# In the expert stage ScalarE rounds all weights and GpSimd only gathers token rows

## What is computed

```
def expert_block(args):
    xb, e = args                                   # 128 token rows, one expert
    hb = jax.nn.silu(xb @ w_gate[e]) * (xb @ w_up[e])
    return hb @ w_down[e]
...
y = lax.map(expert_block, (x_pad, blk_expert))
```

## Time and profile before

| what | value |
|---|---|
| median of 3 runs | 3372.45 us |
| lowest, highest | 3366.57, 3375.68 us |
| the profiled execution, own time | 3378.69 us |
| its span, first to last instruction | 3377.0 us |
| mean granted TensorE clock | 0.90 of full speed |
| busy over the span: PE, DVE, POOL, ACT | 2772.1, 1813.5, 895.6, 883.2 us |
| mean DMA traffic over the span | 130 GB/s |
| first expert stage, from the first load to the next stage's | 1074.7 to 1387.4 us |
| second expert stage | 2899.6 to 3328.8 us |

### The profile page before, as it was taken

One profiled execution on the slowest core, in us unless ns is written; L12 is line 12 of the kernel. 1 busy time (PEld: TensorE's weight loads), 2 busy tenths in 40 slices (PEclk: granted clock), 3 DMA queues, 4 the chain that ended last, 5 costly groups with the idle time before them and its releaser, 6 DMA issues. The chain is left out here.

```text
span 3377.0 us, 36221 instructions
## 1 busy us (share of the span) xinstructions
PE 2772.1 (82%) x11986; PEld 2088.9 (62%) x11986; DVE 1813.5 (54%) x1973; ACT 883.2 (26%) x1395; POOL 895.6 (27%) x692
## 2 busy tenths in 40 slices
PE   5897998999894888368997788888999969488883
PEld 4896665776674767247553455557777758377762
DVE  4394672222234878541365567663654362678884
ACT  3012331000121444221243223321222221134441
POOL 1241002222121676311000000003223211366662
PEclk9898898999996999669898789899999989699996
DMA  2110102111043899835022112112111132599999
GB/s 83 39 44 13 26 20 69 34 40 50 31 151 130 314 352 354 320 111 199 19 67 71 43 53 61 42 44 64 43 37 46 35 114 94 196 355 358 367 352 359
DMA packets 223123, 439.13 MB, mean 130 GB/s; under 512 B 22104, under 2 KB 141224, under 8 KB 215112
## 3 DMA queue, kind: packets, MB, share of 16 engines
q1 hardware_dynamic: 201736, 360.57, 31.4%
q0 software_dynamic: 12960, 47.19, 3.7%
q10 hardware_dynamic: 8352, 30.41, 2.2%
HBM read 343.58 MB, written 90.21 MB: 128 GB/s over the span
## 5 line engine op out<-in xcount | busy, mean ns | idle before, releaser
L1786 DVE TENSOR_TENSOR moe_run_w_low<-moe_run_w,moe_run_w_high 128x2048 fp32r<-128x2048 f32 x174 | 449.0, 2587 | 92.7 <-POOL moe_run_w_high L1646 92.6
L1646 POOL CAST moe_run_w_high<-moe_run_w 128x2048 fp32r<-128x2048 f32 x116 | 300.8, 2600 | 193.6 <-DMA moe_run_w<-w_up 108.9
L134 PE MATMUL rnn_ps<-uT_again_high,rnn_w_high 128*128 128x512 f32 x512 | 206.3, 403 | 29.5 <-ACT rnn_gate L2040 16.0
L134 PE MATMUL rnn_ps<-uT_again_low,rnn_w_high 128*128 128x512 f32 x512 | 203.4, 397 | 0.0
L134 PE MATMUL rnn_ps<-uT_again_high,rnn_w_low 128*128 128x512 f32 x512 | 203.0, 397 | 0.0
L1191 DVE TENSOR_TENSOR merge_gated<-merge_branch,merge_gate 128x512 f32<-128x512 f32 x48 | 33.2, 692 | 304.9 <-ACT merge_gate L1176 304.9
L1675 PE MATMUL moe_run_up<-moe_run_w_high,moe_run_xT_high 128*128 128x512 f32 x464 | 196.5, 423 | 0.0
L1675 PE MATMUL moe_run_up<-moe_run_w_low,moe_run_xT_high 128*128 128x512 f32 x464 | 190.0, 409 | 0.0
L1675 PE MATMUL moe_run_up<-moe_run_w_high,moe_run_xT_low 128*128 128x512 f32 x464 | 189.2, 408 | 0.0
L1661 PE MATMUL moe_run_turn<-all_ident,moe_run_x 128*128 128x128 f32 x464 | 77.6, 319 | 130.7 <-DMA moe_run_x<-v,moe_run_idx 130.6
L134 PE MATMUL merge_gates<-uT_high,merge_wg_high 128*128 128x512 f32 x384 | 171.1, 446 | 13.4 <-POOL merge_wg_low L147 13.4
(11 more groups left out here) (442 smaller groups left out, 6769.3 us busy)
## 6 DMA issues: line engine op xcount, KB each, us to landing
moe_run_w<-exp_w SPq DMA_DIRECT2D x96, 512.0 KB, 7.9
moe_run_w<-w_gate SPq DMA_DIRECT2D x68, 512.0 KB, 7.2
moe_run_w<-w_up SPq DMA_DIRECT2D x68, 512.0 KB, 9.0
moe_run_w<-w_down SPq DMA_DIRECT2D x34, 1024.0 KB, 7.3
moe_y<-moe_run_y ACTq DMA_DIRECT2D x58, 512.0 KB, 6.7
moe_run_w<-exp_w SPq DMA_DIRECT2D x24, 1024.0 KB, 7.1
rnn_raw<-w_in SPq DMA_DIRECT2D x32, 512.0 KB, 3.9
moe_y<-moe_run_zero SPq DMA_DIRECT2D x26, 512.0 KB, 8.7
```

The lines of the kernel that those rows point to most:

```text
L134: last = pe.matmul(out, a, b, start=(k == 0), stop=(k == n - 1))
L1646: pool.tensor_copy(hi[p][j][:], raw[p][j][:]).then_inc(s_hi[j], 1)
L1786: dve.tensor_tensor(lo[p][j][:], raw[p][j][:], hi[p][j][:].bitcast(F32), ALU.subtract).then_inc(s_lo[j], 1)
```

## The change

GpSimd's `gather_and_round` becomes `gather`: it copies the row numbers and issues the gather, and no longer casts. The wait for the turned rows of block b - 2 stays, so a gather is issued as soon as its row buffer is free. ScalarE gets the function `round_up`, with the same waits that GpSimd had for these casts (the raw tile loaded; the products that read the previous contents of the high tile done). In its loop the cast of tile 0 of b + 2 comes first, the cast of tile 1 of b + 2 after `round_rows`, and `round_down` of b + 1 moves from the front of the pass to behind the gate. In the prologue the casts of blocks 0 and 1 stand among the casts of rows, ahead of the first `round_down`. The orders on SP, TensorE and VectorE are as before, and VectorE still waits for `s_hi[j]`.

```diff
--- before.py
+++ after.py
@@ -1627,7 +1627,7 @@
 
             @block.gpsimd
             def _(pool):
-                def gather_and_round(i, p, first):
+                def gather(i, p, first):
                     b = 2 * i + p
                     if not first:
                         pool.wait_ge(s_turn, 2 * b - 2)
@@ -1638,13 +1638,7 @@
                     pool.indirect_dma_start(
                         out=x[p][:], out_offset=None, in_=v_d,
                         in_offset=bass.IndirectOffsetOnAxis(ap=idx[p][:, 0:1], axis=0)).then_inc(s_x[p], 16)
-                    for j, s_used in enumerate((s_half, s_up)):
-                        pool.wait_ge(s_raw[p][j], 32 * i + 32)
-                        if not first:
-                            pool.wait_ge(s_used, b - 1)
-                        pool.sem_inc(s_go, 1)
-                        pool.tensor_copy(hi[p][j][:], raw[p][j][:]).then_inc(s_hi[j], 1)
-                in_order(pool, gather_and_round)
+                in_order(pool, gather)
 
             @block.tensor
             def _(pe):
@@ -1720,6 +1714,12 @@
                 for p in range(2):
                     act.sem_inc(s_st[p], ST0)
 
+                def round_up(i, p, j, first=False):
+                    act.wait_ge(s_raw[p][j], 32 * i + 32)
+                    if not first:
+                        act.wait_ge((s_half, s_up)[j], 2 * i + p - 1)
+                    act.copy(hi[p][j][:], raw[p][j][:]).then_inc(s_hi[j], 1)
+
                 def round_down(i, p, first=False):
                     b = 2 * i + p
                     act.wait_ge(s_raw[p][2], 16 * i + 16)
@@ -1756,18 +1756,24 @@
                     act.wait_ge(s_y, 2 * b + 2 + Y0)
                     act.dma_start(y_d[bass.ds(b * P, P), :], y[p][:]).then_inc(s_st[p], 16)
 
+                round_up(0, 0, 0, True)
                 round_rows(0, 0, True)
+                round_up(0, 0, 1, True)
                 round_rows(0, 1, True)
+                round_up(0, 1, 0, True)
+                round_up(0, 1, 1, True)
                 round_down(0, 0, True)
                 gate(0, 0, True)
                 n = more(act)
                 with act.Fori(0, n) as i:
                     for p in range(2):
                         nxt = (i + p, 1 - p)
-                        round_down(*nxt)
+                        round_up(i + 1, p, 0)
                         round_middle(i, p)
                         round_rows(i + 1, p)
+                        round_up(i + 1, p, 1)
                         gate(*nxt)
+                        round_down(*nxt)
                         store(i, p)
                 round_down(n, 1)
                 round_middle(n, 0)
```

## The result

| | before | after |
|---|---|---|
| median of 4 runs each | 3369.51 us | 3312.83 us |
| lowest, highest | 3365.38, 3375.68 | 3306.35, 3317.87 |
| span of the profiled execution | 3377.0 us | 3304.6 us |

The ratio is 0.9829, 95% interval 0.9804 to 0.9854: 57 us faster, where 45 were forecast. On one of the chips (the first run of early gathers alone, gathers behind the second cast, middle first, down cast first, and the kernel before beside them) part of the executions were in a slower state and are left out of the ratios; the traced one of down cast first is among them, and most of its loss lies ahead of the first expert stage, which it reaches at 1137.9 us where middle first does at 1080.6.

What follows compares the result with a forecast made beforehand. The prediction took the DMA engines to bound the expert stages, with 5% left open; -24.6 us in the steady state and -20 at the starts made -45, so 3334 us profiled or 3327 as median, range 3275 to 3362.

Steps and rivals of the forecast that it cites:

- forecast case: Expert stages: steady blocks and starts both gain, -45 us in all, own range -25 to -65; chance 0.50.
- DMA engines as the bound, 5% open, left open by a loop from landing to reload: Steady expert blocks: DMA share 0.95; landing to next issue falls from 14.15 to 10.8 us, loop to 10.3 per block.
- VectorE freed of GpSimd: VectorE's weight differences: all at 2.28 us once GpSimd no longer casts beside them, an excess of 53 us.
- ScalarE fits, 9.4 to 9.7 us, its waits turn into waits for loads: ScalarE per steady block: with the added casts 9.4 to 9.7 us, below 11.66, its groups waiting for weights, not TensorE.
- the layout: One steady block on ScalarE and VectorE, timed from half 0's landing: copies and store to 9.7, loads issued at 10.8 us.
- At the rate of now: Steady blocks: share 0.99 instead of 0.95 at unchanged transfer rate gives 11.39 and 11.19 us, 24.6 us less.
- the two ends: Steady state: near end, today's rate at share 0.99, 24.6 us less; other end, the loop's 10.3 us at 407 GB/s, 75 less.
- faster transfers too: Rival, steady blocks: a queue never dry moves more per busy us, periods 10.3 to 10.7, 75 to 95 us less; chance 0.17.
- The start, -20 us: Starts of both expert stages: earlier second gather and first reload remove nearly all of the idle 10.6 and 9.4 us.
- Transfers capped near 358 GB/s: Rival, steady blocks: periods stay 11.87 and 11.66 us, only the start's 20 us come, 3352; chance 0.15.
- ScalarE as the bound at 14.1 us: Rival, steady blocks: ScalarE's waits stay beside its 9.7 us of work, +121 less 20, 3473 us; chance 0.11.
- Gathers, "on a full DMA this alone gives nothing": Steady blocks: gathers one block earlier end TensorE's 1.24 us wait for rows, but the same 0.5 MB gives no time.

Runs made afterwards that it cites:

- early gathers alone: Kernel before with each gather issued ahead of the previous block's casts, which stay on GpSimd; ratio to before 0.9900, on a second chip 0.9891 (3339.8 us).
- gathers behind the second cast: Changed kernel with each gather waiting for ScalarE's cast of the previous block's second up half; ratio to before 1.036, some 120 us slower.
- middle first: Changed kernel with the middle's cast ahead of the wait for the next load on ScalarE; ratio to before 0.9894.
- down cast first: Changed kernel with the down cast back at the front of ScalarE's pass, ahead of the wait for the next load; ratio to before 0.9874.
- the idle copies: Changed kernel plus two unused 128 x 1024 copies per block on GpSimd behind each gather: 0.9904, 3346.4 us; with four copies 0.9985, 3371.4 us.
- the extra work: Changed kernel plus two idle casts of 128 x 1024 per block on ScalarE ahead of the copies out; ratio to before 0.9848, 3327.1 us.
- two other orders: Changed kernel with ScalarE's middle cast, or its down cast, moved ahead of the wait for the next load; ratios to before 0.9894 and 0.9874.
- the repeat: The changed kernel again, unaltered, on another chip beside the kernel before; ratio 0.9803, 3308.4 us against 3375.6.

## Why the prediction was right

The sign was right, and 57 us lies in the forecast case's own range of 25 to 65. The total came nearer than its terms did: the steady state was put at half of what came, the start at half as much again, and in the second stage what happened is the rival to which the prediction gave 0.17. By its own steps:

- *DMA engines as the bound, 5% open, left open by a loop from landing to reload.* Right: the time from landing to reload fell to 10.5 us as laid out (10.8) and the share rose to 1.00. The 14.15 us taken for the kernel before was a long block; the medians were 13.9 and 12.8.
- *VectorE freed of GpSimd.* Right: 2.286 us each; the idle copies cost 38 us by sharing alone, and the casts' move behind early gathers brings 31.
- *ScalarE fits, 9.4 to 9.7 us, its waits turn into waits for loads.* Right, by the waits and by the extra work that cost 14 to 19 of 120 us. The order that the layout rested on is part of it: two other orders lose 15 to 30 us.
- *"At the rate of now".* This is the mis-sized term. The steady state was put at 11.39 and 11.19 us, from 0.99 of share at an unchanged rate: -24.6 us. It measured 10.91 and 10.63: -52.0 us. 381 and 391 GB/s lay between the two ends that were weighed (about 370, and 407), and the near end was taken. The second stage, at 10.63 us and 391 GB/s, is inside the rival "faster transfers too" (10.3 to 10.7 us, above 385 GB/s), the first just outside. In the repeat both periods are outside (10.94 and 10.81 us), at 380 and 386 GB/s. The reason given, that casts do not change how fast packets move, is not settled by these runs: the rate over the share did change, 366 GB/s with two idle copies on GpSimd and 387 without, and the cause is open.
- *The start, -20 us.* The mechanism is shown, the term was too large: -7.7 and -5.4 us, 13 in sum (15.5 in the repeat). The first reload was expected at 26.3 us behind the first load and came at 28.3 and 29.7; and around it the DMA engines are still not full (0.94 and 0.86 over 20 us).
- *The errors cancel in part, which is luck:* +27 in the steady state against -7 at the starts, and the pair of traces shows 15 us more than the medians do; so 57 were measured against 45.
- *The rivals.* Transfers capped near 358 GB/s: fallen, 391 GB/s over 330 us. ScalarE as the bound at 14.1 us: fallen in the changed kernel; but 14.6 us per block appear as soon as the gathers stay behind ScalarE's casts.
- *Gathers, "on a full DMA this alone gives nothing".* Wrong. The prediction took TensorE's wait for rows as 1.24 us from one row; over the steady windows it was 31.8 and 46.8 us. Alone they give 36 us, 13.9 of it at the starts (36.0 and 35.1 us shortened to 28.8 and 28.4) and 20 in the steady state (249.2 and 361.3 us to 235.7 and 354.9); and without them the casts' move loses 120.

Open stays why the bytes per busy DMA microsecond differ: 353/0.95 = 372 GB/s before, 391/1.01 = 387 after, 359/0.98 = 366 with two idle copies. The kernels with a later reload have the lower value, but what slows single transfers in them was not taken apart. So the experiments show which parts of the change bring the time, and not why the same transfers then move faster.

## What to carry to other kernels

Where buffers are double and a load follows the last reader, lay out the time from landing to reload, engine by engine in its real order: it sets how early the next load is issued, and here 2.3 to 3.4 us of it went with a gain larger than the DMA engines' idle share had shown. Take it over all blocks and not from one. It does not fix the period by itself: with early gathers alone its medians are 11.8 and 13.4 us, the latter above the 12.8 of the kernel before, and the blocks are shorter all the same (11.23 and 11.45 us). Before work is moved to an in-order engine, ask which loops the new place closes: with each gather behind the casts of the block before, a block took 11.7 to 11.9 us with these casts on GpSimd and 14.6 with them on ScalarE. And put first on that engine whatever only waits for the landing, ahead of all that waits for TensorE; two other orders lost 15 to 30 us here.

## What was not expected of the hardware

DMA shares of 0.98, 0.99 and 1.01 were seen at 359, 372 and 391 GB/s with the same mix of transfers; the share alone did not tell whether anything was left. And a GpSimd copy of 128 x 1024 took 1.05 us alone and 2.88 us beside VectorE's differences of two SBUF tiles, which themselves grew from 2.28 us to between 2.4 and 3.8 us. The Trainium skill (SBUF — State Buffer, SBUF: two separate sides) describes an exclusive lock for a whole instruction between a GpSimd operation and a VectorE one with two SBUF inputs. The rows here agree with it as far as they go: a copy grew by 1.8 us, less than one difference, and a difference by up to 1.5 us, about one copy; the lock itself stands in no row.
